# One layer of a hybrid decoder trunk: memory norm beside the z gate's projection, memory keys and values projected before the delta rule and kept in scratch memory, the RG-LRU recurrence in pairs of tiles

## The reference

```python
qkv, _ = causal_conv(dn_qkv, ...)                    # branch A, gated delta rule
o, dn_s = gated_delta_rule(q, k, v, beta, log_alpha, dn_s0)
out_a = rms_norm(o, w) * silu(dn_z)                  # z: the gate of branch A

xc, _ = causal_conv(lru_x, ...)                      # branch B, RG-LRU
r, i = sigmoid(xc_blocks @ w_r + b_r), sigmoid(xc_blocks @ w_i + b_i)
log_a = -8.0 * r * softplus(-lam)
bx = sqrt(-expm1(2 * log_a)) * (i * xc)
h_t = exp(log_a) * h_(t-1) + bx                      # a scan over the 1024 tokens
out_b = hseq * silu(lru_g)

mn = rms_norm(mem, mem_norm_w)                       # branch M: 256 memory tokens of width 1024
kv = einsum('bmd,de->bme', mn, w_mem_kv)             # 512 key and 512 value columns
mk = rms_norm(mk per head, mem_kn_w)
out_m = softmax(mq @ mk.T) @ mv * silu(mg)

y = x + (sum over branches of sigmoid(gate_n) * (branch_n @ w_branch_n)) @ w_out
```

## Time and profile before

| | |
|---|---|
| median of 3 runs | 1914.81 us (1914.75 to 1919.53) |
| the profiled execution: its own time | 1926.65 us |
| its span, from first to last instruction | 1924.5 us |
| busy: PE | 1735.6 us, 90% of the span |
| busy: DVE, ACT, POOL | 791.4, 539.2, 526.6 us (41%, 28%, 27%) |
| mean granted TensorE clock | 0.944 of full speed |
| moved by DMA | 161.11 MB |

### The profile page before, as it was taken

How to read it: one execution, slowest core, us unless ns; L and a number is a source line. 1 busy time by engine, 2 the same in 40 slices (tenths; PEclk the granted TensorE clock), 3 DMA queues, 4 the chain that set the end, 5 groups by cost and what they waited for, 6 DMA issues and landing times. The chain is left out here.

```text
span 1924.5 us, 26940 instructions
## 1 busy us (share of the span) xinstructions
PE 1735.6 (90%) x11030; PEld 1656.5 (86%) x11030; DVE 791.4 (41%) x1169; ACT 539.2 (28%) x898; POOL 526.6 (27%) x392
## 2 busy tenths in 40 slices
PE   4989897999999997998999999999795969899999
PEld 3989897999999996997988989999785959798977
DVE  4576622333333325603753110444456511653711
ACT  5132222222222221322433222211153132454300
POOL 0324316333334126113452312122110231001410
PEclk9989998999999998998998889999897989899999
DMA  3111033232232154223553212342100332342441
GB/s 124 35 35 44 23 77 73 69 64 73 62 67 57 50 148 121 77 79 93 166 154 117 88 56 82 98 140 66 39 22 17 116 110 66 102 124 67 154 132 61
DMA packets 185335, 161.11 MB, mean 84 GB/s; under 512 B 16992, under 2 KB 153523, under 8 KB 184694
## 3 DMA queue, kind: packets, MB, share of 16 engines
q1 hardware_dynamic: 185214, 159.40, 29.0%
HBM read 130.33 MB, written 29.17 MB: 83 GB/s over the span
## 5 line engine op out<-in xcount | busy, mean ns | idle before, releaser
L234 POOL TENSOR_TENSOR wL<-w_raw,wH 128x1024 fp32r<-128x1024 f32 (+1 forms) x120 | 260.2, 2168 | 962.8 <-ACT wH L227 962.7
L258 PE MATMUL ps<-hH,wH 128*128 128x344 f32 x1920 | 463.3, 351 | 46.7 <-PEq L176 16.0
L258 PE MATMUL ps<-hL,wH 128*128 128x344 f32 x1920 | 419.5, 328 | 0.0
L258 PE MATMUL ps<-hH,wL 128*128 128x344 f32 x1920 | 416.5, 326 | 0.0
L258 PEld LDWEIGHTS ps<-hH,wH 128*128 128x128 f32 x1920 | 329.4, 197 | 68.4 <-issue 50.0
L258 PEld LDWEIGHTS ps<-hL,wH 128*128 128x128 f32 x1920 | 336.1, 196 | 0.0
L258 PEld LDWEIGHTS ps<-hH,wL 128*128 128x128 f32 x1920 | 331.6, 194 | 0.0
L227 ACT ACTIVATE wH<-w_raw 128x1024 fp32r<-128x1024 f32 (+1 forms) x120 | 112.7, 939 | 149.1 <-PE ps L258 93.1
L2308 POOL TENSOR_SCALAR fa_logits<-fa_c_bc,token_scalars 128x128 f32<-128x128 f32 (+7 forms) x32 | 59.8, 1869 | 94.6 <-PE ps L2333 59.7
L2437 DVE SCALAR_TENSOR_TENSOR fa_logits<-ps,fox_rq,fa_logits 128x512 f32<-128x512 f32 (+3 forms) x48 | 28.3, 612 | 121.1 <-POOL fa_logits L2309 66.0
L1395 ACT ACTIVATE d_m<-ps 128x512 f32<-128x512 f32 x48 | 28.6, 595 | 141.9 <-PE ps L1570 141.9
(11 more groups left out here) (555 smaller groups left out, 2842.4 us busy)
## 6 DMA issues: line engine op xcount, KB each, us to landing
w_raw<-in_w_in SPq DMA_DIRECT2D x80, 512.0 KB, 5.0
m_th<-gate_spill SPq DMA_DIRECT2D x28, 516.0 KB, 4.2
gate_spill<-d_gate SPq DMA_DIRECT2D x18, 516.0 KB, 3.0
fa_kv<-in_cache_fox_k SPq DMA_DIRECT2D x32, 256.0 KB, 3.2
fa_kv<-in_cache_fox_v SPq DMA_DIRECT2D x32, 256.0 KB, 3.3
w_raw<-in_w_branch SPq DMA_DIRECT2D x32, 256.0 KB, 2.7
gate_spill<-fa_gate SPq DMA_DIRECT2D x10, 516.0 KB
x_rows<-in_x_prompt SPq DMA_DIRECT2D x8, 512.0 KB, 6.3
```

The source lines that it names most:

```text
L234: pool.tensor_tensor(self.wL[:, t % 2, 0:nk], self.raw[:, t % 2, 0:nk], self.wH[:, t % 2, 0:nk].bitcast(F32), ALU.subtract).then_inc(self. ...
L258: last = pe.matmul(self.ps[:, b + g, 0:cols], w[:, t % 2, k], x[:, k, g * cols:(g + 1) * cols], start=(k == 0 and n == 0), stop=(k == nk - ...
```

## The change

- Memory norm. `memory_norm` goes. A new side `UnitsAndMemory` of the z gate does the same operations: the load of the memory first on SP, the squares before ACT empties tile 1, the reciprocal root and the scaling in DVE's part of tile 1, the 16 transposes in tile 2, two behind each step of k, into PSUM banks 6 and 7 in turn (the third pair on waits for DVE's copy of the pair two before).
- Memory keys and values. The eight tiles of `w_mem_kv` are planned behind `dn_z`. One `project_tiles` with eight tiles stands between the z gate and the delta rule; each result (128 x 256, 128 KB) goes to the new scratch tensor `mem_kv_spill`. The merge of branch B loads all eight back (1 MB) at its end, behind its last weight loads, and SP waits for them. `mem_kT` and `mem_vT` are slices of that buffer.
- The recurrence. `Lru` works in pairs of channel tiles: 12 products in tile 0 and 12 in tile 1 of the projection, two behind each of the steps k = 1 to 6; the square roots before ACT empties tile 2; products and scans of two channel tiles each in DVE's parts of tiles 2 and 3. `dve_last` goes.
- Branches B and M share one gate buffer.

```diff
 class Merge:
@@ sync
         K.loads(sp, self.end + 2)
+        if self.fetch:
+            dst, src, sem = self.fetch
+            sp.dma_start(dst[:], src.rearrange("j p t -> p j t")).then_inc(sem, 16)
+            sp.wait_ge(sem, 16)
...
+class UnitsAndMemory(UnitFactors):
...
+    def sync_first(self, sp):
+        for t in range(2):
+            sp.dma_start(self.X[:, t], self.K.i["mem_prompt"][0, t * P:(t + 1) * P]).then_inc(self.Y["in"], 16)
+
+    def act_before(self, act, j):
+        super().act_before(act, j)
+        Y = self.Y
+        if j == 1:
+            act.wait_ge(Y["in"], 32)
+            for t in range(2):
+                act.activation(self.SQ[:], self.X[:, t], ACT.Square, accum_out=self.M[0][:, t:t + 1]
+                               ).then_inc(Y["sq"], 1)
+                act.wait_ge(Y["sq"], t + 1)
+        if j == 2:
+            for k in range(KD):
+                act.wait_ge(Y["tr"], k + 1)
+                act.activation(self.MH[:, k], self.K.ps[:, 6 + k % 2, 0:MEM], ACT.Identity, scale=self.w(k)
+                               ).then_inc(Y["hi"], 1)
...
+    def pe_part(self, pe, j, k):
+        super().pe_part(pe, j, k)
+        if j != 2:
+            return
+        if k == 0:
+            pe.wait_ge(self.N["d_rows"], 2)
+            pe.wait_ge(self.Y["scaled"], 2)
+        if k >= 2:
+            pe.wait_ge(self.Y["lo"], k - 1)
+        for t in range(2):
+            last = pe.transpose(self.K.ps[:, 6 + k % 2, t * P:(t + 1) * P], self.X[:, t, k * P:(k + 1) * P],
+                                self.K.ident[:])
+        last.then_inc(self.Y["tr"], 1)
...
 class Lru(Side):
     def pe_part(self, pe, j, k):
-        if k < 2:
+        if j >= H // 2 or not 1 <= k < 7:
             return
...
+        for x in range(12 * j + 2 * (k - 1), 12 * j + 2 * k):
+            t, r, g = x // 6, x // 3 % 2, x % 3
+            if x >= 2:
+                pe.wait_ge(N["gate"], x - 1)
+            pe.matmul(K.ps[:, 6 + x % 2, 0:G3], self.BD[:, r, t], K.OT[:, t, g * G3:(g + 1) * G3], start=True,
+                      stop=True).then_inc(N["product"], 1)
...
     def act_before(self, act, j):
+        if j == H // 2:
+            for t in range(H):
+                act.wait_ge(N["u"], t + 1)
+                act.activation(self.U[:, t], self.U[:, t], ACT.Sqrt).then_inc(N["root"], 1)
...
     def act_after(self, act, j):
+        for t in (2 * j, 2 * j + 1):
+            act.wait_ge(N["nla"], t + 1)
+            act.activation(self.U[:, t], self.A[:, t], ACT.Tanh).then_inc(N["th"], 1)
+            act.activation(self.A[:, t], self.A[:, t], ACT.Exp, scale=-1.0).then_inc(N["a"], 1)
...
-    def dve_last(self, dve):
...
-        for t in range(H):
+        for t in range(2 * j - H, 2 * j - H + 2):
             dve.wait_ge(N["root"], t + 1)
...
 def build(nc, ins, outs):
...
+                units = UnitsAndMemory(K, sb, c2)
+                with nc.sbuf_tensor("z_slots", [P, 2, TOK], F32) as GZ:
+                    gate_branch(K, at["dn_z"], "dn_z", GZ, "ga", units, spill=K.d_z)
+                KV = c2.enter_context(nc.sbuf_tensor("mem_kv_T", [P, 2 * H, MEM], F32))
+                t = at["mem_kv"]
+                project_tiles(K, t, 8, None, KV, "mk", x=(units.MH, units.ML), cols=MEM,
+                              stores=[(K.emptied(t + e), K.d_mkv[e], KV[:, e]) for e in range(8)])
...
-                    memory_norm(K, MH, ML)
-                    t = at["mem_kv"]
-                    project_tiles(K, t, 4, None, KX, "mk", x=(MH, ML), cols=MEM)
-                    project_tiles(K, t + 4, 4, None, VX, "mv", x=(MH, ML), cols=MEM)
```

More of the change, by code:

```diff
@@ L1849, in act_before @@
         K, N = self.K, self.N
[L1850 to L1856, removed]
+        if j == H // 2:
+            for t in range(H):
+                act.wait_ge(N["u"], t + 1)
+                act.activation(self.U[:, t], self.U[:, t], ACT.Sqrt).then_inc(N["root"], 1)
+        if j >= H // 2:
+            return
+        for x in range(12 * j, 12 * j + 12):
+            t, r, g = x // 6, x // 3 % 2, x % 3
+            b = PROW[("lru_b_r", "lru_b_i")[r]] + t
+            act.wait_ge(N["product"], x + 1)
+            act.activation((self.A, self.U)[r][:, t, g * G3:(g + 1) * G3], K.ps[:, 6 + x % 2, 0:G3], ACT.Tanh,
+                           scale=0.5, bias=K.hpar[:, b:b + 1]).then_inc(N["gate"], 1)
     def act_after(self, act, j):
         N = self.N
-        act.wait_ge(N["nla"], j + 1)
-        act.activation(self.U[:, j], self.A[:, j], ACT.Tanh).then_inc(N["th"], 1)
-        act.activation(self.A[:, j], self.A[:, j], ACT.Exp, scale=-1.0).then_inc(N["a"], 1)
+        if j >= H // 2:
+            return
+        for t in (2 * j, 2 * j + 1):
+            act.wait_ge(N["nla"], t + 1)
+            act.activation(self.U[:, t], self.A[:, t], ACT.Tanh).then_inc(N["th"], 1)
+            act.activation(self.A[:, t], self.A[:, t], ACT.Exp, scale=-1.0).then_inc(N["a"], 1)
     def act_last(self, act):
         K, N = self.K, self.N
-        for t in range(H):
-            act.wait_ge(N["u"], t + 1)
-            act.activation(self.U[:, t], self.U[:, t], ACT.Sqrt).then_inc(N["root"], 1)
         act.wait_ge(N["hT"], 1)
@@ L2671, in build @@
         K.d_q = dram("decode_q", (NB, H, P))
+        K.d_mkv = dram("mem_kv_spill", (2 * H, P, MEM))
         K.d_z = dram("z_gate_spill", (H, P, TOK))
@@ L2700, in build @@
         plan("dn_z", 4)
+        at["mem_kv"] = len(K.tiles)
+        for e in range(8):
+            K.plan(ins["w_mem_kv"][0, :, e * P:(e + 1) * P].rearrange("(k p) c -> p k c", p=P), KD, "act")
         at["delta"] = len(K.tiles)
@@ L2715, in build @@
         plan_merge(1)
-        at["mem_kv"] = len(K.tiles)
-        for e in range(8):
-            K.plan(ins["w_mem_kv"][0, :, e * P:(e + 1) * P].rearrange("(k p) c -> p k c", p=P), KD, "act")
         plan("mq", 4)
```

121 lines of the change are left out of this document (46 added, 75 removed).

## The result

The changed kernel takes **1892.28 us** (four runs, 1887.65 to 1896.94); the kernel before, in runs beside it, 1914.78 (four runs, 1913.46 to 1919.53). The ratio is **0.9878, with a 95% interval of 0.9848 to 0.9908**, or 22.5 us less between the medians. The forecast was 1894.0, -20.8 us. The profiled execution took 1896.94 us, its span is 1894.9 us and its mean granted clock 0.953 (before 0.944).

A forecast was written before the change was run, and what follows sets the result against it. PE, busy 90% of the span, was taken as the bound. Old memory block -44.4, z gate and new stage +36.7, recurrence -13.1 sum to -20.8 us; from 1914.8 that gives 1894.0 us, range 1885 to 1908 (forecast's own 1888 to 1901).

The forecast's parts named there:

- Place C: Old memory block between branch B's merge and `mq`: 50.7 us of PE removed, 4.3 idle and 2.0 cold added, -44.4 us.
- cold start of `mq`: After the pause behind branch B's merge the clock has fallen, so `mq` starts cold and loses 2.0 us.
- Place A: Z gate to delta rule: transposes and wait +2.2, new memory stage +29.6, pause before the delta rule +4.9; +36.7 us.
- Place B: Recurrence in branch B's gate stage: 16.3 us gained at its end, less stalls of 2.1 and 1.1; -13.1 us.
- The wait of the transposes: End of branch B's gate stage: scans end 7.0 us behind PE's projection, where they ended 23.3 us behind it.
- the stall on ACT: Projection tile 1 of gate stage B: the third product waits for ACT's first Tanh, 2.1 us.
- the meeting with the block weights: Projection tile 0 of gate stage B: the first product, a step earlier, meets the block weights' load, 1.1 us.
- Rival 1: Recurrence fits altogether: POOL's splits miss DVE's two-input operations and neither stall appears; 7.4 us less, 1886.6 us; chance 0.12.
- Rival 2: DMA queue backs up: pause before the delta rule 8 us longer, read-back ends 3 us after its cover; 1905; chance 0.11.
- Rival 3: Recurrence stays in the tail, as when roots come late: none of 16.3 us won, stalls stay; 1910.3 us; chance 0.07.
- Rival 4: Memory norm not beside the z gate's projection: PE waits in tile 2, up to 10 us; 1904 us; chance 0.05.
- Rival 5: Clock stays low across the new stage, 15.6 us, and the delta rule's first chunk, 24 more; 1933.6 us; chance 0.05.

The follow-up runs named there:

- experiment 4: Changed kernel with the 1 MB read-back issued at the start of branch B's merge instead of its end; 1895.63 us, one execution.
- recurrence-only kernel: Kernel before with only the changed kernel's `Lru`, the memory work left where it was; 1904.22 us, ratio 0.9930.
- experiment 3: Changed kernel with seven of the new stage's eight stores issued as each tile is emptied, the eighth at the end; 1899.56 us, one execution.
- experiment 1: Each half alone: kernel before with the new `Lru`, 1904.22 us (0.9930); changed kernel with the old `Lru`, 1906.03 us (0.9946).
- experiment 6: Changed kernel, one edit each: gate stage B's splits on DVE, 1893.63 us; tile 1's products a step later, 1891.17; new stage's splits on DVE, 1892.45.
- experiment 2: Changed kernel with the new stage ending without its store wait, which moves into the delta rule's first chunk; 1895.92 us, ratio 0.9868.
- experiment 5: Kernel before with 8 of its 16 memory transposes, four banks read twice; 1920.62 us, one execution.
- four-edit kernel: Changed kernel with both stages' splits on DVE, tile 1's products a step later, and no store wait ending the new stage; 1882.94 us, ratio 0.9833.

## Why the prediction was right, and where it was off

The forecast held in its sum (-20.8 against -21.8 in the profile and -22.5 between medians) and, unlike a sum that is right by luck, in each of its places.

- **Place C**, -45.8 against -44.4. The pause is 3.88 us for the 4.3 taken, and 1.58 us were lost at the cold start of `mq` for 2.0 (its length in the ten other profiles with the change, 61.8 to 63.1 us, would make it 1.5 to 2.8). The read-back cost nothing, shown by experiment 4. About half a us is the old stretch's own variation (121.01 us in the profile before, 120.42 in the recurrence-only kernel with the same code).
- **Place A**, +37.4 against +36.7. The 16 transposes and the wait of 0.47 us made the third tile 13.69 us where "near 13.6" was written. The eight tiles took 29.4 us for 29.6. The pause was 5.36 us for 4.9, and experiment 3 shows that my reasoning on it was right in kind and wrong in proportion. I gave the store alone 3.6 us of pause and the queue the remaining 1.3; it is 2.7 us without the queue, and another 2.7 are the queue's drain. The two errors cancel, so that the 4.9 was closer than its parts. The estimate by the Trainium skill, page "DMA: Bandwidth & Descriptors", section "Anatomy of one DMA — SWDGE (gpsimd) path", which is for another path than SP's, made 3.9 us of the pause. Neither run agrees: 5.36 with the queue ahead of the store, 2.67 without, and the measurements decide.
- **Place B**, -13.4 against -13.1, alone 13.4 us by experiment 1. The wait of the transposes was forecast at 7.0 us and is 7.05; the stall on ACT 2.1 and is 1.96; the meeting with the block weights 1.1 and is 0.67. That two splits at 2.1 us fall into the chain was the choice with the least behind it, one row; experiment 6 shows it.
- **The rivals.** Rival 1 (all of the recurrence fits) needed POOL's splits to miss DVE; they hit, once on an operation so small that one would not have counted it. Rival 2 (queue) is at work in a small way, 2.7 us of the pause, short of its 8. Rival 3: the roots ended at 1463.2, and DVE never waited for one. Rival 4: the wait at the scaled memory is 0.47 us. Rival 5: in the new stage the clock is 0.50 for the first 4 us and then 1.00; in the delta rule's first chunk the 1.7 us of a cold start are taken up by the next wait, as experiment 2 shows. Its price used 0.24 us for a cold matmul of 256 columns; in the new stage they start 0.21 us apart.
- **Readings of the profile before.** Two were loose and moved no term of the sum. The clock row falls below 9 in 11 of 40 slices, which is more than a few. And against rival 5 I wrote that the clock returned within 4 us at each restart; at the one of the earlier trace rows PE restarts at 1318.08, and the clock is still 0.59 in 1322 to 1324.
- **On the transposes** the Trainium skill's page "TensorE: Matmul & The Clock Gate", section "Part 4: PE-mode transpose", would have had the sum 2 us lower. It is within what the profiles differ by, and experiment 5 doesn't decide it; the earlier trace rows still stand against it. Open.
- **Not forecast**: that the same stages differ by several us between executions. Attention, which no variant touches, took 258.0 to 265.6 us in fourteen profiles. It may be part of the 11.8 us by which the profiled execution of before exceeds its median, since attention at 265.3 us is among the long ones; the rest of these 11.8 us is not explained.

What stays open: why one load of the new stage came late in two of the eleven profiles that have this stage (PE waited 2.52 and 3.56 us). It was not tried to issue the delta rule's rows earlier, although experiment 2 points to them.

## What to carry to other kernels

Moving work from a stage where every engine is idle in turn to one where the tensor engine is busy can be priced from the trace, place by place, if every new stage's pause is priced as well. Here the queue ahead of the last store cost the pause as much as the store's landing and the passage together, 2.7 us each, so all stores but the last are worth issuing as they become ready; read the stage too, since part of the gain went into its tiles. Before expecting a shorter pause to pay, search for the next thing that starts with the stage and doesn't depend on the tensor engine; if it ends later, it takes the gain. When single edits are below what a measurement tells apart, read each in its own stage, then time them together.

## What was not expected of the hardware

- **The clock can fall after the restart, not in the pause.** In the pause of 3.88 us before `mq` the granted clock is 1.00 to its end, and it drops once PE works again. (In a pause of 3.34 us of the kernel before, ahead of 1318.08, it fell within the pause, to a mean of 0.70 in its last 2 us.) Windows of PE, the changed kernel:

```profile
1555.00:1557.00 2.00, 0.00 (x0) 1.00 0.00 0
1557.00:1559.00 2.00, 0.37 (x2) 1.00 0.00 0
1559.00:1561.00 2.00, 2.00 (x12) 0.65 0.61 116
1561.00:1563.00 2.00, 2.00 (x9) 0.50 0.52 146
1563.00:1565.00 2.00, 2.00 (x16) 0.99 0.87 211
```

  Behind the pause of 2.06 us of the four-edit kernel the first 5 us of the delta rule have a mean clock of 0.66, behind that of 1.29 us in experiment 2 it is 1.00 throughout. So the clock inside a pause doesn't tell what the restart will cost.
- **POOL's split costs DVE's small operations as much as its large ones**: 0.14 to 2.30 us on 128x8, 1.23 to 3.33 on 128x1032, while the scan on 128x1024, already running when the split began, kept its 2.29 us; POOL's own split became 3.45 and 4.36 us long in place of 2.4. By the starts and ends under place B this looks like waiting for the other's end, which would make the price what is left of POOL's operation, whatever the size of DVE's. With the splits on DVE all of this is gone, at 1.22 us each.
- **The longest stage differs most between executions.** In attention's second half the mean granted clock was 0.84 to 0.86 in the executions that took 264.3 us and more, 0.88 to 0.92 in those that took 258.0 to 261.3. Here the changed kernel, then that with gate stage B's splits on DVE; same code in this stretch:

```profile
1057.26:1189.96 132.70, 129.08 (x805) 0.86 0.27 84
```

```profile
1050.11:1179.09 128.98, 125.04 (x825) 0.92 0.27 87
```
